# The second layer's cached pages compressed within the first layer, and the decode rows' convolution on VectorE, in a two-layer decoder step

## The reference

```
for l in range(2):                                    # DEPTH
  z = x @ w_in[l]                                     # conv branch, q, k, v, gates
  u = ua * sigmoid(ug)
  conv[t] = sum(u_ext[t + w] * conv_w[w] for w in range(31)) + conv_b     # 512 channels
      # prompt: u_ext = 30 zero rows + u;  decode: u_ext = 30 cached rows + 4 rows, for each sequence
  conv_out = silu(LN(conv)) @ w_conv_out
  k_cmp, v_cmp = compress(cached rows + new rows)     # h = rows in blocks of 32, stride 16, (+ pe) @ w1; gelu(h) @ w2
  attention over k_cmp/v_cmp, over chosen blocks of the cached pages, and over a window of 512
  x = LN1(ALPHA * x + (gate_a * conv_out + gate_b * attn_out) @ w_o)
  x = LN2(ALPHA * x + (silu(x @ w_gate) * (x @ w_up)) @ w_down)            # D_FF 2816
```

## Time and profile before

| | |
|---|---|
| median of 3 runs | 1192.49 us (1191.62 to 1194.08) |
| the profiled execution's own time | 1188.55 us |
| its span in the trace | 1186.7 us |
| PE busy | 1039.2 us (88%), 7438 matmuls |
| PE weight load busy | 965.6 us (81%) |
| DVE busy | 555.3 us (47%) |
| ACT busy | 495.1 us (42%) |
| POOL busy | 770.9 us (65%) |
| transfers | 185.07 MB, mean 156 GB/s |

### The profile page before, as it was taken

The page is one execution under the profiler, slowest core; times in us unless marked ns, Lnnn a source line. Parts: engine busy times, 40 slices in busy tenths (PEclk is TensorE's granted clock), DMA queues, the critical chain, the costliest instruction groups (busy, mean ns, idle before and its releaser), DMA issues.

```text
span 1186.7 us, 22922 instructions
## 1 busy us (share of the span) xinstructions
PE 1039.2 (88%) x7438; PEld 965.6 (81%) x7438; DVE 555.3 (47%) x1070; ACT 495.1 (42%) x902; POOL 770.9 (65%) x1077
## 2 busy tenths in 40 slices
PE   5997798977798999999889968899669799999994
PEld 5996577765787999999779947787558699999993
DVE  2997946435624232210249987543446332222003
ACT  4333345533436544433353232654334364444334
POOL 6998216622493989998559971455127569999882
PEclk9988789988898999999989987999779989999997
DMA  8646458421152664444256534674002324444441
GB/s 305 219 164 216 128 179 281 169 92 54 43 191 82 212 238 163 177 160 169 81 183 219 172 96 133 207 266 174 36 36 102 129 108 160 172 167 160 175 145 76
DMA packets 78140, 185.07 MB, mean 156 GB/s; under 512 B 9283, under 2 KB 42435, under 8 KB 77507
## 3 DMA queue, kind: packets, MB, share of 16 engines
q1 hardware_dynamic: 74130, 171.22, 41.4%
q10 hardware_dynamic: 3744, 11.40, 2.7%
q0 software_dynamic: 144, 0.96, 0.2%
HBM read 170.97 MB, written 12.57 MB: 155 GB/s over the span
## 4 chain that ended last, share of the span: by engine, by line
POOL 63%; issue 35%; POOLq 1%; DMA 1%; ACT 0%; SPq 0%
POOL w_lo L567 57%; POOL hid L590 3%; POOL res L588 2%; POOLq L561 0%; DMA table<-page_table_in 0%; DMA wch<-weights_in 0%; POOLq L585 0%; POOLq L147 0%; POOL hid L588 0%; ACT w_hi L974 0%; POOL hid L591 0%; SPq L429 0%; POOLq L573 0%; SPq L170 0%; POOLq L578 0%
## 5 line engine op out<-in xcount | busy, mean ns | idle before, releaser
L567 POOL TENSOR_TENSOR w_lo<-wch,w_hi 128x256 fp32r<-128x256 f32 x940 | 705.8, 784 | 404.6 <-ACT w_hi L974 402.9
L627 PE MATMUL proj<-x_hi,w_hi 128*128 128x288 f32 x1376 | 416.7, 303 | 39.3 <-DVE x_lo L1598 17.3
L628 PE MATMUL proj<-x_hi,w_lo 128*128 128x288 f32 x1376 | 411.4, 299 | 0.0
L629 PE MATMUL proj<-x_lo,w_hi 128*128 128x288 f32 x1376 | 410.9, 299 | 0.0
L974 ACT ACTIVATE w_hi<-wch 128x1024 fp32r<-128x1024 f32 x235 | 248.3, 1057 | 230.3 <-PE proj L629 118.3
L627 PEld LDWEIGHTS proj<-x_hi,w_hi 128*128 128x128 f32 x1376 | 263.7, 192 | 51.1 <-issue 27.2
L628 PEld LDWEIGHTS proj<-x_hi,w_lo 128*128 128x128 f32 x1376 | 264.5, 192 | 0.0
L629 PEld LDWEIGHTS proj<-x_lo,w_hi 128*128 128x128 f32 x1376 | 263.9, 192 | 0.0
L1295 DVE SCALAR_TENSOR_TENSOR hid<-u_p,sm,hid 128x256 f32<-128x256 f32 x240 | 164.6, 755 | 3.4 <-DVE sq L1324 1.0
L645 PE MATMUL proj<-hid_lo,w_hi 128*128 128x288 f32 x352 | 104.2, 296 | 0.0
L643 PE MATMUL proj<-hid_hi,w_hi 128*128 128x288 f32 x352 | 103.8, 295 | 0.0
(11 more groups left out here) (236 smaller groups left out, 1298.3 us busy)
## 6 DMA issues: line engine op xcount, KB each, us to landing
wch<-weights_in SPq DMA_DIRECT2D x235, 512.0 KB, 3.2
pg<-cmp_pages_in SPq DMA_DIRECT2D x128, 128.0 KB, 2.6
pg<-slc_pages_in SPq DMA_DIRECT2D x128, 128.0 KB, 2.1
wn<-win_in SPq DMA_DIRECT2D x4, 2048.0 KB, 8.4
win_out<-wn ACTq DMA_DIRECT2D x4, 2048.0 KB, 8.1
hid<-w_in SPq DMA_DIRECT2D x2, 1024.0 KB, 5.9
kv_out<-kv ACTq DMA_DIRECT2D x2, 864.0 KB, 5.4
res<-xT_in SPq DMA_DIRECT2D x1, 1152.0 KB, 5.1
```

The costliest lines, as they stand in the source:

```text
L567: last = nc.gpsimd.tensor_tensor(lo[:, cols], raw[:, cols], hi[:, cols].bitcast(F32), ALU.subtract)
L627: mm(ps, hi[:, kb], x_hi[:, kb], start=kb == 0, stop=False)
L628: mm(ps, lo[:, kb], x_hi[:, kb], start=False, stop=False)
L629: last = mm(ps, hi[:, kb], x_lo[:, kb], start=False, stop=kb == KD - 1)
```

## The change

**The layers are written out.** The loops over layers are gone, each engine's stream holds layer 0 and then layer 1, and semaphore targets are constants. The loads and low parts that the loop issued past the last layer are gone too.

**The decode rows' convolution goes to DVE.** For each channel block: one multiplication of 128x992 (8 sequences, 4 rows, 31 taps, read as overlapping spans of u) into scratch, one sum over the taps, one addition of the bias. All four blocks stand after the fourth `take_u` and before `convolve(50)`.

**Layer 1's compression of cached pages goes into layer 0.** The bias stands between the two statistics of layer 0's LN1 and `compress(0)` after them; `compress(1)` and `compress(2)` stand after pairs 4 and 11 of the channel mixer, `second(0)` to `second(2)` after pairs 6, 12 and 19; `compress(3)` is split, 5 matmuls before and 11 after LN2's second statistics; `second(3)` is in layer 1 after out 5. ACT's and DVE's steps are put between pairs by tables. In layer 1 all taps after the rotation of q and k stand in one run, `convolve(56)`, and the gates' projection waits for `cmp_ready(4)`.

**Transfers.** w1 and pe get their place in the window's tile, so the window of each layer is loaded when w1 is no longer in use (it waits for `h_done(5)`, that is `compress(4)`): it is issued behind pages 3 to 5. Layer 1's tiles 0 to 3 are loaded in layer 0, four pages to a chunk for four chunks each time, at w_o's second chunk and at the channel mixer's chunks 7, 19 and 31. Layer 1's window moves from layer 0's channel mixer into layer 1; its past u moves to the first down chunk. `take_u` no longer waits for w1 and w2.

```diff
+HOIST_H = {4: 1, 11: 2}
+HOIST_SECOND = {6: 0, 12: 1, 19: 2}
+HOIST_ACT = {0: ("copy", 0), 2: ("square", 0), 4: ("tanh", 0), 7: ("out", 0), 6: ("copy", 1), 8: ("square", 1), 10: ("tanh", 1),
...
+HOIST_DVE = {1: ("sum", 0), 3: ("poly", 0), 5: ("gate", 0), 7: ("sum", 1), 9: ("poly", 1), 11: ("gate", 1),
...
-        w1_sb = gate_b.rearrange("p k t -> p (k t)")[:, 0:2 * KD * P].rearrange("p (a c w) -> p a c w", a=2, c=KD)
+        w1_sb = wn[:, 0:2].rearrange("p a (c w) -> p a c w", c=KD)
...
             def load_window(layer, gr):
                 wait_alone(*gpv_done(layer, gr))
+                if gr == 0:
+                    wait_alone(*h_done(layer, 5))
...
-                if first:
-                    load_window(layer, 0)
...
                     if j == EARLY + AHEAD - 1:
-                        for i in range(3, 6):
+                        for i in range(3, 6) if layer == 0 else ():
                             load_pages(layer, i)
+                        load_window(layer, 0)
...
-                    if more and 0 <= n < 2 * PAGES:
-                        load_pages(layer + 1, 0, n, 1)
-                    if more and n == 2 * PAGES:
-                        load_window(layer + 1, 0)
-                        load_past(layer + 1)
+                    if more:
+                        if j == CHUNKS - CH_DOWN:
+                            load_past(layer + 1)
+                        if j == CH_IN + CH_MIX + 1:
+                            load_compress(layer + 1)
+                        for i, at in enumerate((CH_IN + CH_MIX + 1, FIRST_GU + 7, FIRST_GU + 19, FIRST_GU + 31)):
+                            if 0 <= j - at < 4:
+                                load_pages(layer + 1, i, 4 * (j - at), 4)
...
-                for tap in range(CONV_W):
-                    dst = tap_s[:] if tap else out
-                    do(nc.gpsimd.tensor_tensor(dst, u_s[:, :, :, tap:tap + DEC_T], tap_weight(conv_w[:, :, tap]), ALU.mult))
-                    if tap:
-                        do(nc.gpsimd.tensor_tensor(out, out, tap_s[:], ALU.add))
...
+            def convolve_sample(c):
...
+                windows = bass.AP(at.tensor, at.offset, [at.ap[0], [TAIL + DEC_T, DEC_B], [1, DEC_T], [1, CONV_W]])
...
+                do(v.tensor_tensor(sample_p, windows, taps, ALU.mult))
+                do(v.tensor_reduce(out, sample_p, AX, ALU.add))
...
                         for n in range(2 * KF):
                             project_x(layer, O_GU + n, CH_IN + CH_MIX + CH_WO + n, KD if n == 0 else None)
+                            if more and n % 2:
+                                if n // 2 in HOIST_H:
+                                    compress(layer + 1, HOIST_H[n // 2])
+                                if n // 2 in HOIST_SECOND:
+                                    second(layer + 1, HOIST_SECOND[n // 2])
...
+                    if more and which == 0:
+                        compress_bias(layer + 1)
+                    elif more:
+                        compress(layer + 1, 3, 0, 5)
                     statistics(layer, KD, sqv, k("mean_d"), lambda kb: pe.wait_ge(*squared(layer, 3 + 4 * which + kb // 2)))
+                    if more and which == 0:
+                        compress(layer + 1, 0)
+                    elif more:
+                        compress(layer + 1, 3, 5, 16)
```

More of the change, by code:

```diff
@@ L447, in load_pages @@
             def load_pages(layer, i, first=0, n=2 * PAGES):
-                slot = i % PG_SLOTS
-                if first == 0:
-                    user, back = before(i, 8, PG_SLOTS)
+                slot = page_slot(layer, i)
+                if first == 0 and page_before(layer, i):
+                    there, user = page_before(layer, i)[-1]
                     sig, count = page_user(user)
-                    wait_alone(*sig(layer, count - back * sig.per_layer))
+                    wait_alone(*sig(there, count))
                 source = cmp_pages if i < 4 else slc_pages
@@ L682, in statistics, with compress_bias, compress @@
                 stat_done.up(last)
-            def compress(layer, i):
+            def compress_bias(layer):
+                pe.wait_ge(*cmp_in(layer, 3))
+                pe.wait_ge(*spread_read(layer, 0))
+                for c in range(2):
+                    for sp_ in range(8):
+                        last = mm(ps_g[:, 2 * c:2 * c + 2], w1_sb[:, c, sp_], pe_emb[c][:, sp_], start=sp_ == 0, stop=sp_ == 7)
+                bias_done.up(last)
+            def compress(layer, i, first=0, end=16):
                 if i == 4:
@@ L838, in group_turn @@
                 gout_turned.up(pe.transpose(ps_o[:, P:2 * P], group_rows, k("ident")))
-            with layers(pe) as layer:
+            for layer in range(DEPTH):
                 state["out"] = 0
+                more = layer + 1 < DEPTH
                 for o in range(8):
                     project_x(layer, o, o, -KD if o == 0 else None)
+                    if layer and o == 5:
+                        second(layer, 3)
                 pe.wait_ge(*nsa_ready(layer, 1))
                 pe.wait_ge(*uo_ready(layer, 0))
+                if layer:
+                    pe.wait_ge(*cmp_ready(layer, 4))
                 for kb in range(KD):
@@ L862, in _ @@
                     fill(layer)
-                for c in range(2):
-                    for sp_ in range(8):
-                        last = mm(ps_g[:, 2 * c:2 * c + 2], w1_sb[:, c, sp_], pe_emb[c][:, sp_], start=sp_ == 0, stop=sp_ == 7)
-                bias_done.up(last)
-                compress(layer, 0)
-                compress(layer, 1)
-                second(layer, 0)
-                compress(layer, 2)
-                second(layer, 1)
+                if layer == 0:
+                    compress_bias(layer)
+                    compress(layer, 0)
+                    compress(layer, 1)
+                    second(layer, 0)
+                    compress(layer, 2)
+                    second(layer, 1)
                 for i in range(6):
@@ L892, in _ @@
                 v_turned.up(pe.transpose(ps_s[0:32, 1, P:2 * P], kv[:, VSL, SEQ:TOK], k("ident")))
-                compress(layer, 3)
-                second(layer, 2)
+                if layer == 0:
+                    compress(layer, 3)
+                    second(layer, 2)
                 fill(layer)
-                second(layer, 3)
+                if layer == 0:
+                    second(layer, 3)
                 compress(layer, 4)
@@ L982, in do @@
                 if wait:
-                    act.wait_ge(*sig(now["layer"], n))
+                    act.wait_ge(*sig.nth(n))
             def read_out(o, out, func, wait=False, **kw):
@@ L1090, in _ @@
                 high_part(0, n)
-            hi_ready.count = 0
-            with layers(act) as layer:
+            for layer in range(DEPTH):
                 now["layer"] = layer
@@ L1108, in chunk_read @@
                     high_part(layer, o + PAIRS)
+                more = layer + 1 < DEPTH
+                if layer:
+                    h1_copy(layer, 3)
                 for n in range(KC):
@@ L1279, in do @@
                 if wait:
-                    dve.wait_ge(*sig(now["layer"], n))
+                    dve.wait_ge(*sig.nth(n))
             def read_out(o, i, wait=True):
@@ L1472, in group_out @@
                     do(v.tensor_copy(dst, src), go_ready if g else None)
-            with layers(dve) as layer:
+            for layer in range(DEPTH):
                 now["layer"] = layer
                 dve.wait_ge(*past_in(layer, 1))
-                dve.wait_ge(*small_in(layer, 3))
+                dve.wait_ge(*small_in(layer, 1))
                 dve.wait_ge(*conv_stored(layer, 0))
@@ L1489, in _ @@
                 now["tap_at"] = {}
+                more = layer + 1 < DEPTH
+                if layer:
+                    compress_sum(layer, 3)
                 take_u(0)
+                if layer:
+                    compress_poly(layer, 3)
                 nsa_f = s("nsa").rearrange("p (c w) -> p c w", c=KD)
@@ L1495, in _ @@
                 take_u(1)
+                if layer:
+                    compress_gate(layer, 3)
                 convolve(8)
@@ L1499, in _ @@
                 take_u(3)
+                for c in range(KC):
+                    convolve_sample(c)
                 convolve(50)
@@ L1620, in _ @@
                                 low_hidden(i - 1)
+                            if more and i in HOIST_DVE:
+                                step, tile_ = HOIST_DVE[i]
+                                {"sum": compress_sum, "poly": compress_poly, "gate": compress_gate}[step](layer + 1, tile_)
                         low_hidden(KF - 1)
@@ L1629, in _ @@
                     center(layer, 1 + which, resv, KD)
+                    if which == 0 and more:
+                        compress_bias_dve(layer + 1)
                     normalise(layer, 1 + which, resv, KD)
```

293 lines of the change are left out of this document (173 added, 120 removed).

## The result

The changed kernel takes 1219.34 us (median of 4 runs, 1211.95 to 1223.76), the kernel before 1192.21 (1191.62 to 1194.08). The ratio is 1.0225, 95% interval 1.0196 to 1.0255: 27 us slower, where the forecast was 11.9 and the range ended at 1213. The direction was right, the size was not. The profiled execution took 1216.7 us, its span is 1214.9, which is 28.2 more than before. Its runs also lie 12 us apart, where those of the kernel before lay within 2.5 at that time.

What follows compares the result with a forecast made beforehand. The prediction took PE to bound layer 0's mixer and DVE layer 1's head. Its terms summed to +11.9 on the profiled 1188.55, 1200.5; adding 3.94 for the median gave 1204, range 1187 to 1213.

Steps and rivals of the forecast that it cites:

- 14.1, 2.4, 1.3 and -1.2: Layer 0's PE: two compress in mixer, three second, LN1's additions, and window load leaving the mixer; in us.
- Rival 1: Layer 0's mixer: POOL is the bound, so inserted matmuls cost nothing; -16.5 from the sum, median 1187.9; chance 0.15.
- Four terms, 9.7 in sum: Layer 0's page bursts delay weight chunks: +3.3 at chunks 19 and 31 each, +1.0 at 7, +2.1 at w_o.
- reserve of 4.2 us: Layer 0's mixer: chunk lateness absorbed before PE loses time, taken from one late chunk; subtracted from a burst's 7.5.
- +2.1 at w_o: Layer 0's output weights: cost in us of the page burst there, same sum with a larger reserve.
- LN2's +0.6: Layer 0's LN2: cost in us of compress(3), 5 matmuls against a wait and 11 in a gap.
- the chain from `take_u(3)`: Layer 1's head: DVE's new order from 634.9 ends at 714.7, bringing the conv statistics 21.0 us sooner.
- the step on layer 0: Layer 0's scores: late window makes PE wait, then half clock, +6.0 (bounds 3 to 8); decode convolution hidden under it.
- The tail of layer 1, put at 0: Layer 1, conv statistics to output projection: no change, 0.
- The written-out layers**, booked at 0: Loop bookkeeping over layers: register instructions hide behind earlier work; 0, at most -4.
- a rival: Loop's turn and SP's waiting branches: straight code shortens waits by about 8 us, median 1196.4; chance 0.10.
- My reading of it: DVE's decode convolution beside POOL: multiplications pay twice, reductions nothing; 15.5 us instead of 13, head's end 1.2 later.

Runs made afterwards that it cites:

- Experiment 2: Changed kernel with layer 1's pages loaded two to a chunk for eight chunks, and the mixer's compressions two pairs later; 1204.95 us.
- Experiment 5: Changed kernel with only tiles 0 and 1 hoisted, no compress in the mixer, pages two to a chunk, layer 0's window early; 1186.51 us.
- experiment 9: Kernel of Experiment 5 with SP's small page-load loop written out; 1175.04 us.
- experiment 10: Changed kernel with only SP's page-load loop written out; 1202.87 us.
- experiment 11: Kernel before with only SP's page-load loop written out; 1185.42 us.
- experiment 6: Kernel before with the decode rows' convolution moved to DVE; 1194.39 us.
- experiment 7: Kernel before with its loops over layers written out, order on each engine unchanged; 1193.43 us.
- experiment 8: Kernel of experiment 1 with layer 0's pages of tiles 3 to 5 loaded for 64 of 128 rows; 1220.11 us.
- experiment 1: Changed kernel with layer 0's w1 and pe back in gate_b's memory, so its window loads ahead of the pages of tiles 3 to 5; 1216.66 us.
- experiment 4: Changed kernel with the decode rows' convolution back on POOL; 1227.59 us.
- experiment 12: Kernel of Experiment 5 with the decode rows' convolution back on POOL; 1199.77 us.

## Why the prediction was wrong

By the table above, the sum of 11.9 missed 16.7 us: 7.1 in layer 1's tail, 5.6 in LN1 and mixer, 3.4 in layer 0, 1.9 in w_o, less 1.3 in layer 1's head. In two of these the mechanism was wrong or missing (layer 0, the tail); in the others a size was off.

**The mixer, right in kind.** Matmuls put into a busy PE cost their full time. Experiment 2 leaves 19.9 us of LN1 and mixer; the terms were 14.1, 2.4, 1.3 and -1.2, in sum 16.6. The difference lies in LN1: from its first statistics to the mixer's first matmul PE takes 15.5 us before and 20.4 in experiment 2 (18.7 in the changed kernel), where I had +1.3. The mixer behind it takes 14.9 us more, against terms of 15.3. Experiment 5 shows one more side: taking two `compress` and two `second` out, 15.7 by the terms, gives 16.0. Rival 1, POOL as the bound, is refuted: PE's time grew by what was put in.

**The bursts, mis-sized.** Four terms, 9.7 in sum, taken from a reserve of 4.2 us. Experiment 2 measures 9.9 in LN1 and mixer and 3.7 in w_o, 13.6. In proportion the term "+2.1 at w_o" was the most wrong: w_o's first burst follows a load of w1, pe and w2, and ACT waited 2.40, 3.96 and 5.05 us for three chunks in a row. The mixer's were 7.6 against 9.9.

**Layer 1's head, right in sum.** -20.4 with LN2's +0.6, measured -21.7, and the chain from `take_u(3)` was 78.4 against 79.8. Its parts cancel to some degree: the decode convolution took 11.4 us (12.7 in layer 0) against 13, the 50 taps behind it 36.1 against 32.8, the last 56 taps 22.3 against 24.5. That these last taps ran at 0.40 us was not because POOL was quiet. It had a chunk's low part under way, which was not done until they were:

```profile
739.36 20.62 POOL L602 TENSOR_TENSOR w_lo<-wch,w_hi 128x256 fp32r<-128x256 f32 x4 [19.32 <-ACT w_hi L1021]
```

**What failed as a mechanism is the step on layer 0.** I wrote that the window's landing sets the end of layer 0's scores, that its wait costs 6.0, and that the decode convolution there "is hidden under this wait", with a gain of about 1.5 us at the conv statistics. The pages were not given a cost, because PE had never waited for them before. But in the kernel before, the issue of tile 5's pages ends at 164.64, 0.3 us after PE's first page scores begin: they had no margin. PE reached the conv statistics 5.6 us sooner than before and the scores 5.5 us sooner, stood for 5.97 and then 3.08 us, and the half clock followed: +14.1 to the second scores, where experiments 9 to 11 have 68.7 to 68.9, no loss at all. The profiles of experiments 6 and 7 show that it needs neither the moved window nor the hoisting: each brings PE there 2.4 to 2.9 us sooner by a part of the change alone, and PE waits 2.4 to 3.3 us for pages. Experiment 10 shows that the same page order with the loop written out removes both waits. Of the gain, nothing arrived: +9.4 to the output projection, against 6.0.

**The tail of layer 1, put at 0, is +7.1** from the conv statistics to the output projection. Of it 2.0 come from where I cut the head. Before, DVE's last tap ended at 732.6, and it was PE's own `compress(4)` that held the statistics until 735.76, while DVE made its copies and part of the gelu (timeline of PE, kernel before):

```profile
728.91 7.03 PE L691 MATMUL ps_w<-sq,hid 128*128 128x32 f32 x32
```

Now the copies stand behind the last taps. The prediction took the whole of that head for DVE's. Another 3.7 go with the clock. In the changed kernel's profile the stretch behind the first unit's scores has it at 0.72, in that of experiment 10, the same program there, at 1.00 (busy time, first the changed kernel, then experiment 10):

```profile
794.00:804.00 10.00, 8.87 (x119) 8.10 (x121) 2.63 (x7) 4.80 (x16) 5.62 (x9) 0.72 0.31 107
```

```profile
784.00:794.00 10.00, 9.73 (x157) 9.26 (x158) 4.38 (x12) 3.68 (x15) 7.02 (x11) 1.00 0.44 128
```

From the first to the second decode scores of layer 1 it takes 72.6 us against 68.9. Experiments 2 and 8 have 72.7 and 72.6, experiments 1 and 4 68.8 and 68.7. The last 1.4 us are not assigned. Why an execution gets the low clock there stays open. Over whole executions of the changed kernel the mean granted clock goes with the time: 0.938 in the one of 1211.95 us, 0.934 at 1216.70, 0.926 at 1221.97 and 1223.76.

**The written-out layers**, booked at 0, are 0 (experiment 7). The Trainium skill, Runtime: NRT & Kernel Launch, "Instruction fetch mechanics", ties the forced fetch to a taken branch whose target lies outside the window of two pages of instructions that is loaded; the prediction left this condition out. At the turn of the loop over layers, which I held as a rival, no run here shows a cost. What cost time was a loop that the prediction did not look at, over four page loads on the engine that sets the pace. Its body is short, so the Trainium skill's rule does not foretell a fetch there, and no run separates the branch from the register work of the turn. Together a turn is worth 0.8 to 1.0 us: 32 page loads take SP 36.7, 35.7 and 35.6 us in experiments 9 to 11 instead of 43.1, 43.6 and 43.1, with 8 turns fewer.

**The decode convolution** was only costed on DVE. It is worth 0 in the kernel before, 8.3 in the changed one and 13.3 in experiment 5: the change's two parts are not additive. By the traces of experiments 4 and 12 it is worth most where, without it, DVE's unbroken taps meet a low part that PE needs soon.

## What to carry to other kernels

An edit that makes an engine arrive sooner is worth something only if what it meets is early too: for each gain, look up when the transfers behind the next wait are issued and how much margin they have, even where the trace shows no wait. Work moved into a stage costs its full time if the engine is busy throughout, so move it into gaps and leave the rest: two tiles in two LayerNorms' gaps, with their pages spread and the window early, were 6 us faster than the kernel before, four tiles with the same care 10 slower. With the page loop written out in both, two tiles were 10.4 us faster (1175.04 against 1185.42). In a queue that issues small transfers by a loop, compare the pace inside a turn with the pace over turns before taking it for bandwidth.

## What the hardware showed that I had not expected

- A product of two SBUF tensors (128x992) took 1.18 us three times on DVE while POOL was at w_lo without a pause (from 50.04 on), no more than when it was not; the one before them, at 48.15, took 1.75 beside POOL. A tap of 256 elements beside the same work takes 0.84 instead of 0.41, and the bias' addition on 32 elements went from 0.24 to 0.77:

```profile
54.56 1.18 DVE L1448 TENSOR_TENSOR sq<-u_s,sm 128x992 f32<-128x992 f32 x1
55.78 1.19 DVE L1449 TENSOR_REDUCE hid<-sq 128x32 f32<-128x992 f32 x1
57.00 0.77 DVE L1450 TENSOR_SCALAR hid<-hid,sm 128x32 f32<-128x32 f32 x1
```

  The Trainium skill, VectorE: DVE Perf Modes, "Two Vector instructions with no wait between them", names an interface that an operation on two SBUF tensors shares with GpSimd, but gives no times. My reading of it, that the product pays twice and the bias' addition less, is not what the rows show; no run here says why.
- DVE and POOL do not always share. Beside DVE's 44 taps at 0.84 us in the kernel before, POOL's low-part instructions take 0.88 us each; beside 56 taps at 0.40 us in the changed kernel, POOL has one low part under way from 740.0 to 757.2, and a chunk's four take 20.62 us instead of 2.84. What decides between the two no run here shows.
- Halving the rows of 48 page transfers quickened neither SP nor the kernel. Writing out the small loop that issues them ended the issue 13 to 16 us sooner and made three kernels 7 to 17 us faster.
